# A two-layer streaming encoder in fp32: stage heads re-ordered, two projections finished by thirds of the tokens, last gate products on VectorE, four output buffers

## The chip, the cores and the metric

The kernel runs on one core of one Trainium2 chip. The metric is the device time of one execution in microseconds (us), taken as a median over several runs. The engines are TensorE (PE, its weight loads PEld), VectorE (DVE), ScalarE (ACT), GpSimd (POOL), and SyncE (SP), which only issues DMA here.

## The reference, cut to what matters

Two groups of tokens, 1024 of a new stream and 8 x 16 of running streams, are put side by side as 1152 columns and go through two layers with shared weights, d_model 1024, all in fp32.

```
for layer in range(2):
    h = rms_norm(x, norm_mix[layer])
    mix = ab_mixer(h, ...) if layer == 0 else chunk_mlp_mixer(h, ...)   # each ends in a projection to 1024
    x = x + mix
    h = rms_norm(x, norm_ffn[layer])
    a, gate = split(h @ w_in_ffn[layer])                                # 1024 -> 2 x 2816
    x = x + (gelu(causal_dwconv3(a)) * gate) @ w_out_ffn[layer]         # 2816 -> 1024
y = rms_norm(x, norm_final)
```

The outputs are y for both groups, and the recurrent, pooling and convolution states.

## The kernel before, in words

**Layout.** x lies transposed: eight tiles `xs[:, d, :]` (d = 0 to 7) of 128 channels by 1152 tokens. Token columns are cut into thirds of 384 (tb = 0 to 2) for the projections and into halves of 576 (T1S, T2S) for the feed-forward part. Every fp32 product is made of three fp32r products: an operand is split by ACT into a high part (a copy, `high`, `up_high`, `combo_high`, `w_high`, `y_high`) and by DVE into a low part (a subtraction, `low`, `up_low`, `combo_low`, `w_low`, `y_low`), and TensorE does high x high, high x low and low x high. So each weight piece and each data tile passes through ACT and then DVE before TensorE can use it.

**Order of the work.** There is no scheduler: each engine has a program written out by hand, runs it strictly in order, and waits on counting semaphores. An instruction that waits holds up everything behind it on its engine. SP issues all loads and stores in one such order too.

**Stages.** (1) mixer AB; its output projection is the stage "abo": tiles d = 0 to 5 are done whole (`abo_unit`, all three thirds, three matmuls to a weight block) and tiles 6 and 7 by thirds (`abo_group(d, tb)`, called by `by_token_block`, L1062 on). (2) `ffn(0)`. (3) stage "v" (`v_group`), then the u units, which alternate with `down` steps of mixer C; the last two pairs of channels go through `last_down` (stage "u9"): tiles 0 to 3 whole, tiles 4 to 7 by thirds (`group(d, tb)`, 12 matmuls of 384 columns each, L1054). (4) `ffn(1)`. (5) the final norm, one 128-token tile after another (`finish`, `final`, `store_out`), through two buffers `otok`.

**The end of a projection and the head of ffn.** For each finished group DVE adds the bank to `xs` (`add_down`, L1775), ACT squares it (`tail_sq`), and POOL adds the square to a sum (`add_square`, L3610). `norm_block(l, tb, ssq)` sums over partitions on TensorE (L1078; for tb 1 and 2 the last tile's square is added there, L1082), and ACT makes the reciprocal root (`rms`, L2824 and L2827). With blocks 0 and 1 known, DVE multiplies T1S by it (`normed`, L2239), and forms operands. The ffn is a Strassen-like scheme: 7 products instead of 8 for each pair of blocks, for the up part in 22 pairs n (`head_product(pos)`, pos 0 to 13, for the first two, `product` for the others; 24 matmuls of 288 columns each, L1524), for the down part in 7 products j of 11 steps (`down_step(r, f)`, r = 0 to 76, L1605). The head needs from DVE the sums and low parts of the seven x operands (`combo_sum` L2257, `combo_low` L2264), the weights' sums and low parts (`up_sum`, `up_low` L2235, in a ring of three places that come free with f_done), and the first bank evictions (`head_evict`, among them c22, L2291). The old x is stored to `x_scratch` in DRAM before `normed` overwrites it (waits on x_moved, x_moved_late) and is read back in the down part.

**From the up part to the down part.** A product gelu(conv) x gate of two 128 x 1152 blocks is made by POOL for every two pairs (`y_prod(i)`, i = 0 to 10, L3754), and SP stores it (`store_y(i)`, L791) and later reads halves of it back as y operands (`y_tiles`, L847). `step_weights(r)` (L843) loads the weights of step r, eight places in rotation. The last two products (i = 10) can be made only after the last up product; SP waits for them in `store_y(STEPS - 1)` at r = 6.

**Stage v.** `v_group(c, r)` multiplies 8 weight pieces k with three token tiles; for c = 0 pieces 6 and 7 go to places `va`, which lie over `xs` tile 0, so ACT waits for xl_ready before it writes them (L2811). The norm sums (`norm(2, ssq_v)`) stand behind `v_group(0, 0)`.

## Time and profile before

| | us |
|---|---|
| median of the three runs shown | 2722.01 (2717.48, 2722.01, 2722.22) |
| the profiled execution, its own time | 2718.93 |
| its span, first to last instruction | 2717.2 |
| PE busy in it | 2641.2, 97% |
| DVE, ACT, POOL busy | 1852.8 (68%), 938.0 (35%), 392.4 (14%) |
| mean granted TensorE clock | 0.993 of 2.4 GHz |
| DMA | 249 MB, mean 92 GB/s |

TensorE is busy for all but 76 us of the span. A view by windows of 1 us shows where the rest lies: 6.5 us at the start, stretches of 1 to 4 us around 504 to 555, 1020 to 1068, 1288, 1931 to 1973 and 2438 to 2487, and the last 23 us, in which it has only transposes.

### The profile page before, as it was taken

To read this page: it belongs to the slowest core of one execution; us is meant where nothing else is said; L and a number is where in the kernel's file an instruction comes from. 1 tells how busy PE (TensorE), PEld (TensorE's weight loads), DVE (VectorE), ACT (ScalarE), POOL (GpSimd) and SP (SyncE) were. 2 spreads that over 40 slices of the span, in tenths; PEclk is the share of its full clock that TensorE was granted. 3 is DMA by queue.
4 is the path that set the end of the run, shared out by engine and by line. 5 is a ranking of instruction groups with operands and counts; after the bars stand their busy time and mean duration, and the time that the engine had idled before them with its cause. 6 is when DMAs were issued, how large, how long until landed. Compare 5 with 4: busy or idle time off the path is not lost. (4 is left out here: it accounts for less than half of the span.)

```text
span 2717.2 us, 45387 instructions
## 1 busy us (share of the span) xinstructions
PE 2641.2 (97%) x17820; PEld 2567.2 (94%) x17820; DVE 1852.8 (68%) x3057; ACT 938.0 (35%) x1550; POOL 392.4 (14%) x299
## 2 busy tenths in 40 slices
PE   9999999899999998999999999999899999999998
PEld 8999999899999998999888999999899999999997
DVE  3558883687677778789223765555787777677787
ACT  4414553433232333445222221222532323334443
POOL 3134324201010100000000331001201111110000
PEclk9999999999999999999999999999999999999999
DMA  5111001322222337633111111111222222338533
GB/s 152 39 32 55 25 21 47 108 61 82 65 87 69 107 129 260 226 125 118 40 52 58 36 44 40 42 42 52 96 77 82 65 82 73 108 135 284 196 128 128
DMA packets 233346, 249.01 MB, mean 92 GB/s; under 512 B 13179, under 2 KB 171332, under 8 KB 232900
## 3 DMA queue, kind: packets, MB, share of 16 engines
q1 hardware_dynamic: 233124, 246.36, 27.8%
q8 instruction: 132, 2.16, 0.3%
q14 instruction: 58, 0.48, 0.1%
q10 hardware_dynamic: 32, 0.01, 0.0%
HBM read 202.12 MB, written 44.20 MB: 91 GB/s over the span
## 5 line engine op out<-in xcount | busy, mean ns | idle before, releaser
L1524 PE MATMUL banks<-cx,fh 128*128 128x288 f32 x2816 | 488.1, 295 | 8.8 <-ACT fh L3239 6.4
L1524 PEld LDWEIGHTS banks<-cx,fh 128*128 128x128 f32 x2816 | 413.1, 189 | 11.3 <-ACT fh L3239 7.8
L1524 PE MATMUL banks<-cw,fh 128*128 128x288 f32 x2112 | 368.3, 296 | 12.4 <-issue 6.1
L1524 PEld LDWEIGHTS banks<-cw,fh 128*128 128x128 f32 x2112 | 312.6, 190 | 13.7 <-issue 6.9
L1524 PE MATMUL banks<-cx,fl 128*128 128x288 f32 x1408 | 303.4, 297 | 0.0
L1605 PE MATMUL banks<-ysh,fh 128*128 128x288 f32 x1232 | 264.4, 296 | 17.0 <-DVE ysl L2410 13.2
L1605 PE MATMUL banks<-ysl,fh 128*128 128x288 f32 x1232 | 262.6, 294 | 0.0
L1605 PE MATMUL banks<-ysh,fl 128*128 128x288 f32 x1232 | 262.5, 294 | 0.0
L3754 POOL TENSOR_TENSOR gate<-gate,cv 128x1152 f32<-128x1152 f32 x44 | 120.6, 2742 | 926.3 <-DVE gate L2321 618.5
L3239 ACT ACTIVATE fh<-fraw 128x512 fp32r<-128x512 f32 x220 | 138.3, 631 | 319.1 <-PE banks L1524 264.6
L1524 PE MATMUL banks<-cw,fl 128*128 128x288 f32 x1056 | 228.8, 298 | 0.0
L1524 PEld LDWEIGHTS banks<-cx,fl 128*128 128x128 f32 x1408 | 225.4, 189 | 0.0
L1605 PEld LDWEIGHTS banks<-ysh,fh 128*128 128x128 f32 x1232 | 196.2, 188 | 20.3 <-issue 11.9
L2235 DVE TENSOR_TENSOR fl<-fraw,fh 128x512 fp32r<-128x512 f32 x220 | 152.4, 694 | 82.9 <-ACT fh L3239 82.9
L2803 ACT ACTIVATE wh<-raw 128x512 fp32r<-128x512 f32 x110 | 69.3, 630 | 403.2 <-PE banks L987 220.9
L1605 PEld LDWEIGHTS banks<-ysl,fh 128*128 128x128 f32 x1232 | 196.8, 188 | 0.0
L1605 PEld LDWEIGHTS banks<-ysh,fl 128*128 128x128 f32 x1232 | 196.6, 188 | 0.0
L1755 DVE TENSOR_TENSOR wl<-raw,wh 128x512 fp32r<-128x512 f32 x110 | 88.1, 801 | 125.3 <-ACT wh L2803 125.3
L1524 PEld LDWEIGHTS banks<-cw,fl 128*128 128x128 f32 x1056 | 170.2, 190 | 0.0
L1775 DVE TENSOR_TENSOR xs<-banks,xs 128x384 f32<-128x384 f32 x192 | 95.7, 550 | 91.2 <-PE banks L1012 46.1
L3604 POOL TENSOR_TENSOR raw<-raw,vec 128x512 f32<-128x512 f32 x72 | 84.8, 1183 | 461.2 <-DMA raw<-in_w_uv_c 380.8
L3305 ACT ACTIVATE fh<-flf 128x512 fp32r<-128x512 f32 x110 | 69.6, 633 | 212.0 <-DVE flf L2393 211.8
(417 smaller groups left out, 5312.1 us busy)
## 6 DMA issues: line engine op xcount, KB each, us to landing
fraw<-in_w_out_ffn SPq DMA_DIRECT2D x264, 256.0 KB, 3.4
fraw<-in_w_in_ffn SPq DMA_DIRECT2D x176, 256.0 KB, 4.1
y_scratch<-gate SPq DMA_DIRECT2D x44, 576.0 KB, 2.8
raw<-in_w_uv_c SPq DMA_DIRECT2D x64, 256.0 KB, 2.7
yb<-y_scratch SPq DMA_DIRECT2D x10, 1440.0 KB, 8.7
raw<-in_w_in_ab SPq DMA_DIRECT2D x40, 256.0 KB, 2.9
raw<-in_w_out_c SPq DMA_DIRECT2D x32, 256.0 KB, 2.6
x_scratch<-xs SPq DMA_DIRECT2D x10, 576.0 KB, 6.6
```

Source lines behind the costliest of these rows:

```text
L1524: mm = pe.matmul(bank[:, M0 + c * CH:M0 + (c + 1) * CH], w[:, pos % RING, k * P:(k + 1) * P], x[:, m, part, c * CH:(c + 1) * CH], start=fi ...
L1605: mm = pe.matmul(psp[f][:, M0 + c * CH:M0 + (c + 1) * CH], w[:, f * P:(f + 1) * P], x[:, r % RINGD, c * CH:(c + 1) * CH], start=kk == 0 an ...
L1755: dve.tensor_tensor(wl[:, s % 2, :], raw[:, s % RAWS, :], wh[:, s % 2, :].bitcast(F32), ALU.subtract)\
L1775: dve.tensor_tensor(xs[:, d, tbs(tb)], ps[sg % BANKS][:, 0:TB], xs[:, d, tbs(tb)], ALU.add)\
L2235: dve.tensor_tensor(fl[:, pos % RING, :], src, fh[:, pos % RING, :].bitcast(F32), ALU.subtract)\
L2803: act.activation(wh[:, s % 2, :], raw[:, s % RAWS, :], ACT.Copy).then_inc(w_high_ready, 1)
L3239: act.activation(fh[:, pos % RING, :], src, ACT.Copy).then_inc(f_high, 1)
L3305: act.activation(hi, src, ACT.Copy).then_inc(f_high, 1)
L3604: pool.tensor_tensor(r, r, g, ALU.mult).then_inc(w_scaled, 1)
L3754: pool.tensor_tensor(gate[:, c, :], gate[:, c, :], cv[:, c, :], ALU.mult)\
```

## The change

- Stage abo: tiles 0 to 4 whole, tiles 5, 6 and 7 by thirds. Stage u9: all eight tiles by thirds, so each group (d, tb) takes both parts a = 0 (yh4, yl4) and a = 1 (yh3, yl3) in turn.
- The weights of these groups get places of their own (`tail_place`), and squares four buffers instead of eight.
- Stores of old x: tiles 0 and 1 earlier, the tail tiles of a third in one store, in u9 all eight tiles a third.
- Head of ffn: DVE's and ACT's orders are changed (below), `up_sum` well ahead of its `up_low`.
- The last two gate products move from POOL to DVE, at r = 5 and 8; `store_y(STEPS - 1)` from r = 6 to 12, the read of y blocks 20 and 21 from r = 9 to 14.
- Stage v: pieces 6 and 7 of c = 0 go to new places `ve`, without the wait for xl_ready; the added squares come later, and `norm(2, ssq_v)` moves into `v_group(0, 1)` before k = 5.
- The end: four buffers `otok`; tiles in the order 5, 6, 7, 8, 0 to 4; the transposes of the first three stand between the last down steps of f = 1, 2, 3.
- POOL no longer forwards w_scaled piece by piece in abo and u9, and restores `xs` (xh + xl) two tiles at a time, done by tile 2.

```diff
 PLAN.add("ab", 40, 60, 80)
-PLAN.add("abo", 16, 24, 30)
+PLAN.add("abo", 16, 24, 29)
...
 PLAN.add("uu", 4, 6, 8)
-PLAN.add("u9", 8, 24, 26)
+PLAN.add("u9", 8, 24, 24)
...
-            return ((vb_h, vb_l) if c else (vd_h, vd_l), (wh, wl), (vc_h, vc_l), (va_h, va_l))[k // 2], k % 2
+            return (((vb_h, vb_l), (wh, wl), (vc_h, vc_l), (va_h, va_l)) if c else
+                    ((vd_h, vd_l), (wh, wl), (vc_h, vc_l), (ve_h, ve_l)))[k // 2], k % 2
 
         V_TILES = (6, 7, 8, 3, 4, 5, 0, 1, 2)
         V_SQUARES = tuple((d, 1) for d in range(KD)) + tuple((d, 0) for d in (4, 5, 6, 7, 0, 1, 2, 3))
-        SUMMED_SQ = {0: 18, 1: 48}
-        TAKEN_SQ = {0: 18, 1: 50}
-        TAIL_D = {0: 6, 1: 4}
+        SUMMED_SQ = {0: 15, 1: 36}
+        TAKEN_SQ = {0: 15, 1: 38}
+        TAIL_D = {0: 5, 1: 0}
         V_SUMMED, V_TAKEN = 22, 24
...
+            if l:
+                box, e = (tail_c, i) if i < 3 else (tail_b, i - 3) if i < 7 else (tail_a, 0)
+            else:
+                box, e = (tail_b, i) if i < 4 else (tail_a, i - 4)
+            return box[:, e, 0, :], box[:, e, 1, :]
 
         def v_added(s):
 
...
+            def store_x(d):
+
+                sp.wait_ge(acc_free, PLAN.at["abo"][1] + NTB * (d + 1))
+                sp.dma_start(xscr[0][d], xs[:, d, :]).then_inc(x_moved, 16)
...
-                for d in range(first):
-                    sp.wait_ge(acc_free, g0 + NTB * (d + 1))
-                    sp.dma_start(xscr[l][d], xs[:, d, :]).then_inc(x_moved, 16)
-                sp.wait_ge(pe_tick, t0 + (14 if l else 24))
+                if l == 0:
+                    for d in range(2, first):
+                        store_x(d)
+                sp.wait_ge(pe_tick, t0 + (0 if l else 20))
                 pair_blocks(1)
                 if l:
                     sp.wait_ge(pe_tick, PLAN.at["u9"][2])
...
+                back = xscr[l].rearrange("d p t -> p d t")
+                for a, b in ((0, 1), (1, 2), (2, 3)) if l else ((0, 2), (2, 3)):
+                    sp.wait_ge(acc_free, g0 + NTB * first + b * (KD - first))
+                    sp.dma_start(back[:, first:KD, a * TB:b * TB], xs[:, first:KD, a * TB:b * TB])\
+                        .then_inc(x_moved_late if b == NTB else x_moved, 16)
                 for n in range(2, PAIRS):
                     if n < 4:
...
-                    if r == 6:
+                    if r == 12:
                         store_y(STEPS - 1)
                     if r == 7:
                         y_tiles(yb22[:, 5:9, :], 16, 20, T2S, y_back[2])
                     if r == 20:
                         store_tails(l)
-                    if r == 9:
+                    if r == 14:
                         sp.wait_ge(y_saved[0], 16 * 12 * (l + 1))
-                        y_tiles(yb22[:, 9:11, :], 20, 22, T2S, y_back[2])
+                        y_tiles(yb22[:, 9:11, :], 20, 22, T2S, y_back[0])
                     if r in (13, 15):
                         d = r - 13
-                        sp.wait_ge(x_moved, 176 * l + 144)
+                        sp.wait_ge(x_moved, x_moves(l, X_STORES[l] + 1))
                         sp.dma_start(xs[:, d:d + 2, :], xscr[l][d:d + 2].rearrange("d p t -> p d t"))\
...
+                def group(d, tb):
+
+                    e = KD * tb + d
+                    q, dd = divmod(d, 2)
+                    acc_bank(g + e, g + e)
                     for a, (sh, sl) in enumerate(parts):
-                        if q == 0:
+                        if e == 0:
                             pe.wait_ge(yh_ready, done - 2 + 2 * a)
                             pe.wait_ge(yl_ready, done - 2 + 2 * a)
                         pe.wait_ge(w_high_ready, n + 2 * q + a + 1)
                         pe.wait_ge(w_low_ready, n + 2 * q + a + 1)
...
-
-                def group(d, tb):
-
-                    e = 12 + 4 * tb + d - 4
...
             def abo_group(d, tb):
 
-                e = 18 + 2 * tb + d - 6
+                e = 15 + 3 * tb + d - 5
...
+            def finish(i):
+
+                t = FIN_TILES[i]
+                if i < 4:
+                    pe.wait_ge(d_out, 28 + 24 + i + 1)
+                else:
+                    pe.wait_ge(y_out, i - 3)
+                for d in (4, 5, 6, 7, 0, 1, 2, 3):
+                    if i == 4 and d < 4:
+                        pe.wait_ge(d_out, 28 + 24 + d + 1)
+                    mm = pe.transpose(psp[i % 4][:, d * P:(d + 1) * P], xs[:, d, t * P:(t + 1) * P], ident[:, :])
+                mm.then_inc(fin_turned, 1)
             def ffn(l):
...
+                            if l and j == 6 and last == STEPS and f:
+                                finish(f - 1)
 
...
+                    if c == 0 and r == 1 and k == 5:
+                        norm(2, ssq_v)
                     (high, low), place = v_place(c, k)
...
             v_group(0, 0)
             pe.wait_ge(d_out, 28)
-            norm(2, ssq_v)
 
             def mixing_matrix(m):
...
-                at_first(2, first, KD - 1 - l)
+                at_first(2, first, 3 if l else 6)
                 dve.wait_ge(rstd_ready, NTB * 2 * l + 2)
-                dve.wait_ge(x_moved, 176 * l + 16 * KD)
+                dve.wait_ge(x_moved, x_moves(l, X_STORES[l]))
                 for d in range(4):
                     normed(d, T1S)
-                at_first(2, KD - 1 - l, KD - 1)
-                combo_low(0, 0)
-                combo_low(0, 1)
-                at_first(2, KD - 1, KD)
-                combo_low(0, 2)
-                combo_low(0, 3)
+                for k in range(4):
+                    combo_low(0, k)
+                    if l and k in (1, 3):
+                        at_first(2, 3 + k // 2, 4 + k // 2)
+                    if l == 0 and k == 1:
+                        at_first(2, 6, 7)
                 normed(4, T1S)
                 normed(5, T1S)
+                if l == 0:
+                    at_first(2, 7, 8)
                 combo_low(2, 0)
+                if l:
+                    at_first(2, 5, 6)
                 normed(6, T1S)
                 combo_low(2, 1)
+                if l:
+                    at_first(2, 6, 7)
                 normed(7, T1S)
                 combo_low(2, 2)
+                if l:
+                    at_first(2, 7, 8)
                 combo_low(2, 3)
                 up_low(3)
                 dve.wait_ge(rstd_ready, NTB * (1 + 2 * l))
-                dve.wait_ge(x_moved_late, 96 if l else 32)
+                dve.wait_ge(x_moved_late, 16 * (l + 1))
                 for d in range(4, KD):
                     normed(d, T2S)
+                up_sum(4)
                 dve.wait_ge(convc_mm, l + 1)
                 for k in range(4):
                     combo_low(6, k)
-                up_sum(4)
                 up_low(4)
+                up_sum(5)
                 for d in range(4):
                     normed(d, T2S)
+                up_low(5)
                 combo_sum(4, 2)
...
+                combo_sum(3, 3)
+                up_low(6)
                 for k in range(4):
                     combo_low(3, k)
-                for pos in (6, 7):
-                    up_sum(pos)
-                    up_low(pos)
+                up_sum(7)
                 for k in (0, 1, 3):
                     combo_sum(4, k)
+                up_low(7)
                 for k in range(4):
                     combo_sum(1, k)
+                up_low(8)
                 for k in range(4):
                     combo_low(4, k)
-                for n in range(2):
-                    head_evict(n, "d")
-                    up_low(8 + n)
+                head_evict(0, "d")
+                up_low(9)
                 for k in range(4):
                     combo_sum(5, k)
+                head_evict(1, "d")
+                up_low(10)
                 for k in range(4):
                     combo_low(1, k)
-                for n in range(2):
-                    head_evict(n, "a")
-                    up_low(10 + n)
+                head_evict(0, "a")
+                up_low(11)
+                head_evict(1, "a")
                 for k in range(4):
                     combo_low(5, k)
                 up_low(12)
-                up_low(13)
                 dve.memset(apad_a[:, 0:2], 0.0)
                 dve.memset(apad_b[:, 0:2], 0.0)
-                up_evict(10)
+                head_evict(0, "c22")
+                up_low(13)
+                head_evict(0, "c12")
                 for pos in range(12, UPS):
                     if pos + 2 < UPS:
                         up_sum(pos + 2)
...
-                conv_part(STEPS - 1, 1, 1)
+
+                def last_product(o):
+
+                    c = conv_half(STEPS - 1, o)
+                    dve.wait_ge(gelu_done[l], 2 * (STEPS - 1) + o + 1)
+                    if o:
+                        dve.wait_ge(up_act_out, on_act(l, PAIRS - 1, C11))
+                    dve.wait_ge(up_dve_out, on_dve(l, PAIRS - 1, (C21, C12)[o]))
+                    dve.tensor_tensor(gate[:, c, :], gate[:, c, :], cv[:, c, :], ALU.mult).then_inc(y_formed[l], 1)
                 for r in range(2, DOWNS):
                     j, kk = divmod(r + 1, STEPS)
...
+                    if r < 5:
+                        conv_part(STEPS - 1, 1, r - 1)
+                    if r in (5, 8):
+                        last_product(r // 8)
...
+                    v_low(V_N + 6)
+                    v_low(V_N + 7)
                     for s in range(8, 16):
                         x_low(s)
-                        if s > 8:
-                            add_square(s)
-                        if s == 13:
-                            v_low(V_N + 6)
-                            v_low(V_N + 7)
+                    for s in range(9, 16):
+                        add_square(s)
...
-            u_groups(7, 1, g3 + 3, t3 + 6)
             n2, g2, t2 = PLAN.at["u9"]
-            low(n2 + 1, n2 + 1)
+            tail_low(1, n2, 0)
+            u_groups(7, 1, g3 + 3, t3 + 6, lambda: tail_low(1, n2 + 1, 1))
+            tail_low(1, n2 + 2, 2)
             y_low(7, yh3, yl3)
-            finish_down(n2, g2, t2)
+            for i in range(3, 8):
+                tail_low(1, n2 + i, i)
...
+                if d == 4:
+                    act.wait_ge(xs_init, KD)
+                    for i in range(6):
+                        tail_high(0, n0 + 10 + i, i)
...
                         x_high(s)
-                    for s in range(10, 14):
-                        v_square(s)
-                    act.wait_ge(xl_ready, 24 + 14)
                     v_high(V_N + 6, 0)
                     v_high(V_N + 7, 0)
-                    v_square(14)
-                    v_square(15)
+                    for s in range(9, 16):
+                        v_square(s)
...
-                    u_gelu((p - 3) // 2, g3)
+            u_gelu(0, g3)
+            act.wait_ge(yl_ready, 12)
+            tail_high(1, n2, 0)
+            tail_high(1, n2 + 1, 1)
+            u_gelu(1, g3)
+            tail_high(1, n2 + 2, 2)
             uy_high(7, yh3)
-            n2, g2, t2 = PLAN.at["u9"]
-            finish_down(n2, g2, t2)
+            act.wait_ge(pe_tick, t2)
+            act.preload_act_table_set("natural_log_exp_and_others")
+            for i in range(3, 8):
+                tail_high(1, n2 + i, i)
...
+            pool.wait_ge(w_scaled, n0 + 4)
+            pool.sem_inc(w_scaled, 12)
+            for d in range(5):
+                for tb in range(NTB):
+                    e = NTB * d + tb
+                    add_square(e, e, sq_e[:, e % 2, :], tb, ssq_e)
+                if d < 3:
+                    restore(2 * d + 2)
+                    restore(2 * d + 3)
...
-                for i in range(STEPS):
+                for i in range(STEPS - 1):
```

## Rows read from the trace of the kernel before

**Rows 1.** The page, costliest groups: DVE's adds of projection groups.
```profile
L1775 DVE TENSOR_TENSOR xs<-banks,xs 128x384 f32<-128x384 f32 x192 | 95.7, 550 | 91.2 <-PE banks L1012 46.1
```

**Rows 2.** Waits of PE, 1008 to 1075: total us, times, longest.
```profile
PE banks L1605 <- DVE ysl L2410: 5.7, 3, 2.1
```

**Rows 3.** Waits of PE, 2430 to 2490.
```profile
PE banks L1605 <- DVE ysl L2410: 5.1, 3, 2.6
```

**Rows 4.** Timelines of DVE, POOL and SP, 1008 to 1072: start, us, what.
```profile
1018.09 3.21 DVE L2410 TENSOR_TENSOR ysl<-yb,ysh 128x576 fp32r<-128x576 f32 x1
...
1017.71 2.96 POOL L3754 TENSOR_TENSOR gate<-gate,cv 128x1152 f32<-128x1152 f32 x1 [31.24 <-DVE gate L2321]
...
1027.37 8.29 SPq L791 DMA_DIRECT2D y_scratch<-gate  x2
```

**Rows 5.** Timelines of ACT, PE and DVE, first head, 500 to 575.
```profile
500.28 1.15 ACT L3239 ACTIVATE fh<-fraw 128x512 fp32r<-128x512 f32 x2 [6.89 <-DMA fraw<-in_w_in_ffn]
...
507.18 0.91 PE L1078 MATMUL banks<-ssq_e,ones 128*128 128x384 f32 x2 [2.34 <-POOL ssq_e L3610]
...
512.74 0.69 PE L1511 MATMUL banks<-ident,crow 128*128 128x128 f32 x4
...
574.80 0.69 PE L1524 MATMUL banks<-cx,fh 128*128 128x288 f32 x4
...
509.95 3.01 DVE L2239 SCALAR_TENSOR_TENSOR xs<-xs,vec,rstd 128x576 f32<-128x576 f32 x4 [3.52 <-ACT rstd L2827]
...
522.88 3.00 DVE L2239 SCALAR_TENSOR_TENSOR xs<-xs,vec,rstd 128x576 f32<-128x576 f32 x4
...
567.81 0.28 DVE L2291 TENSOR_TENSOR apad_b<-banks,u 128x128 f32<-128x128 f32 x1
```

**Rows 6.** Waits of DVE in the first head, 509.9 to 569.
```profile
DVE fl L2235 <- ACT fh L3239: 3.1, 5, 0.7
```

**Rows 7.** Timelines of PE, DVE and POOL, second head, 1919 to 1994.
```profile
1922.77 0.91 PE L1078 MATMUL banks<-ssq_b,ones 128*128 128x384 f32 x2 [0.58 <-POOL ssq_b L3610]
...
1930.43 0.69 PE L1511 MATMUL banks<-ident,crow 128*128 128x128 f32 x4
...
1993.55 0.69 PE L1524 MATMUL banks<-cx,fh 128*128 128x288 f32 x4
...
1926.94 3.80 DVE L2239 SCALAR_TENSOR_TENSOR xs<-xs,vec,rstd 128x576 f32<-128x576 f32 x4
...
1927.66 1.01 POOL L3610 TENSOR_TENSOR ssq_b<-ssq_b,sq_t 128x384 f32<-128x384 f32 x1 [3.25 <-ACT sq_t L3179]
```

**Rows 8.** Windows: us, then PE, PEld, DVE, ACT, POOL busy (count), clock, DMA, GB/s.
```profile
600.00:650.00 50.00, 50.00 (x381) 50.00 (x380) 36.39 (x59) 15.28 (x23) 5.42 (x2) 1.00 0.21 67
...
1700.00:1750.00 50.00, 50.00 (x288) 50.00 (x287) 25.61 (x46) 9.89 (x16) 4.16 (x4) 1.00 0.14 42
...
1290.00:1295.00 5.00, 4.95 (x15) 3.94 (x16) 3.28 (x5) 0.92 (x2) 0.00 (x0) 0.66 0.34 108
...
1921.00:1926.00 5.00, 4.42 (x22) 3.57 (x21) 0.56 (x1) 2.88 (x6) 2.57 (x3) 1.00 0.80 315
```

**Rows 9.** Timelines of DVE and PE where stage u9 begins, 1880 to 1886.
```profile
1881.14 2.62 DVE L2730 TENSOR_TENSOR yl<-work,yh 128x1152 fp32r<-128x1152 f32 x2
...
1883.86 0.76 PE L1036 MATMUL banks<-yh,wh 128*128 128x384 f32 x3 [0.47 <-issue]
```

**Rows 10.** Timeline of PE, stage v, 1284 to 1298.
```profile
1290.05 0.47 PE L1647 MATMUL banks<-va_h,xh 128*128 128x512 f32 x1 [2.18 <-ACT va_h L2811]
```

**Rows 11.** Timelines of PE, ACT and DVE, the end, 2690 to 2717.
```profile
2693.89 3.96 PE L1744 MATMUL banks<-ident,xs 128*128 128x128 f32 x32
...
2695.27 1.03 ACT L3414 ACTIVATE fin_sq<-banks 128x1024 f32<-128x1024 f32 x1 [11.69 <-PE banks L1744]
...
2696.80 1.02 ACT L3414 ACTIVATE fin_sq<-banks 128x1024 f32<-128x1024 f32 x1
...
2712.88 1.28 DVE L2565 SCALAR_TENSOR_TENSOR otok<-banks,fin_sums,fin_gain 128x1024 f32<-128x1024 f32 x1 [1.13 <-DMA out_y_prompt<-otok]
```

More of the change, by code:

```diff
@@ L109, in build @@
         tails_stored = sem("tails_stored")
-        vout_stored = sem("vout_stored")
-        y_stored = [sem(f"y_stored{i}") for i in range(2)]
+        y_stored = [sem(f"y_stored{i}") for i in range(4)]
         w_scaled = sem("w_scaled")
```

305 lines of the change are left out of this document (121 added, 184 removed).

## The prediction, made before the changed kernel was run

> **What bounds the kernel.** The table's busy shares come first: TensorE is busy 97% of the span, so a change can win only what lies in its 76 us of idle time, in windows at half clock, and in the tail without matmuls. The windows of 1 us then say where the idle time is, and the waits and timelines say which instruction ended each stretch. The change touches five places.
>
> *Going down in ffn.* TensorE waits 5.7 us in three stalls in the first ffn and 5.1 in the second [rows 2, 3]. In the first stall DVE's low part of a y operand is started at 1018.09 and ends at 1021.30, just after POOL's gate product of 1017.71 to 1020.67 [rows 4]: the two don't run side by side. The other two stalls follow SP: it is held for 8.29 us from 1027.37 in the store of the last products [rows 4], with the weights of step 7 and on queued behind it.
>
> *The heads of ffn.* In the first, weight pieces of pair 1 come late, ACT waits 6.89 us for them to 500.28, DVE's adds of groups stand behind that, and TensorE waits 2.34 us before norm block 1 [rows 5]. From the end of the projection (E = 512.74, where the tap transposes begin) to the start of product 14 (574.80) it takes 62.1 us [rows 5]; 14 products of 24 matmuls at 50 us for 380 are 44.2 us [rows 8]. DVE is busy nearly all that time and is the bound; it is itself idle 3.1 us in five waits for ACT's high part between its sum and its low part [rows 6]. The second head is alike: E = 1930.43, product 14 at 1993.55, 63.1 us, after a wait of 0.58 us [rows 7].
>
> *Stage v*: 2.18 us of waiting for a high part of weights [rows 10], and then half clock. *The end*: the first transposes start at 2693.89, the last output tile is made at 2712.88 to 2714.16 [rows 11].
>
> **The clock.** The granted clock over 1290 to 1295 is 0.66, a fall to the 1.2 GHz level for part of it, after the 2.18 us idle; it costs 5 x (1 - 0.66) = 1.7 us [rows 8, 10]. Where DVE is the bound such a fall is hidden, elsewhere it adds.
>
> **Part by part.**
>
> *Last gate products to DVE, stores later.* POOL is gone from the place, SP is not held at r = 6. The three stalls go: 5.7 + 5.1 = 10.8 us. DVE gets two more products, each as long as two 576-column operations, at 3.01 for four [rows 5] 1.5 us; it has slack there, as one step of TensorE is 24 matmuls, 3.16 us [rows 8], and its own three operations take under 2.3. The stall on the tail rows' copies is untouched. If DMA were the limit the second and third stalls would return: bounds 10.8 and 3.2 (the first stall alone, 1.6 twice). I take 10.8, since the eight weight places give four steps, 12.6 us, for a load.
>
> *First head.* The tail is 9 groups of 24 matmuls of 384 columns, at 50 us for 288 each 4.17 us [rows 8], and norm block 1 stands two groups before E, not one. The weights of pair 1 load after tile 4, long before they are needed: 2.34 us saved. Norm block 1 at E - 8.3, add, square, two ACT operations: `normed` can start at E - 5.9, against 509.95 = E - 2.8 before. From there to the T2S multiplications DVE took 12.9 us [rows 5]; less the one wait of 0.3, plus one more add of 0.5 [rows 1], plus 0.7 for two square additions of POOL now beside it, 13.8: they start at E + 7.9. From there to the end of c22 it took 568.09 - 522.88 = 45.2 us [rows 5]; less the other waits, 2.8 [rows 6] and 0.1, and `up_low(13)`, 0.6, now behind it, 41.7. Product 12 starts there, product 14 6.3 us later: E + 55.9 against E + 62.1. With the 2.3, 8.5 us. Bounds: 5 if only the start moves, 11 if nothing of POOL is felt.
>
> *Second head.* All 24 groups by thirds, 12 matmuls, 2.08 us each; norm block 1 stands seven groups before E. `normed` can start when (2, 2) is added, E - 9.8. DVE's way to T2S is 12.9 - 0.3 plus four more adds, 14.6. But five square additions of POOL, 1.01 us each, now fall into it. Before, one made four multiplications take 3.80 instead of 3.01 [rows 5, 7], another cost about half of that; I take 0.6 each, 3.0. The add of (7, 2), 1.4 before the end of this, is done at E + 6.4. Only then can the last third of all eight tiles be stored, 1.57 MB, as much as moved in 1921 to 1926 [rows 8]: 4.6 us with the issue, and DVE waits for it before T2S: E + 11.0. Then 41.7 and 6.3: E + 59.0 against 63.1, 4.1; with the 0.6 of norm block 1, 4.7 us. Bounds: 7.5 without POOL's interference, 1.5 with a store of 6.6 us and full blocking.
> The Trainium skill (SBUF — State Buffer, Who interferes with whom) says that a VectorE instruction with two SBUF inputs and a GpSimd one that reads SBUF exclude each other for the whole instruction. The pair at 1018 agrees. By that rule each addition costs DVE its whole 1.01 us, five cost 5.0, and the sum below would be 2.0 lower.
>
> *Entry of u9.* What is new and bad: before, TensorE did 36 matmuls with yh4 (6.25 us, at 50 for 288 [rows 8]) before it needed yh3 and yl3, which are finished at 1881.14 + 2.62 = 1883.76, and waited 0.47 [rows 9]. Now the first group has 6 such matmuls, 1.04 us, and then waits in order for the same pair; one `tail_high` and one `tail_low` of some 0.6 (less than the 0.75 of 576 columns [rows 5]) stand in that way too, one leaves it. So 6.25 - 1.04 + 0.47, and 0.6 on top: a wait of 6.3 us, 5.8 more, and a fall of the clock, 1.7: -7.5 us. Bounds -4.5 (part of the work earlier, no fall) and -9.
>
> *Stage v.* The wait of 2.18 goes and with it the fall: 3.9 us. The x lows of T1S end about 1 us before `v_group(0, 1)` needs them. The norm is ten microseconds later; the first bank is evicted some 0.7 us before `v_group(0, 2)` wants it. Bounds 2.5 and 4.
>
> *The end.* ACT's pitch is 1.53 us a tile [rows 11], DVE's pair of buffers made it 2 (it waited 1.13 for a store [rows 11]). Tile 0 of the new order reaches ACT at about 2692.1, tiles 1 and 2 at 2694.7 and 2697.3 between the down steps, the other six follow at 1.53: the last output tile ends 3.0 us after ACT starts it (its own 1.53, DVE's 1.28, and 0.2 between), at 2709.6 against 2714.2: 4.6 us. Bounds 3 and 5.5.
>
> *At nothing:* restores, w_scaled, `x_scratch` stores of abo, the loop of u units. They lie under TensorE's full stretches (12.5 us a tile against 9 us of POOL), and would show as a wait in abo if that cover were too short.
>
> **The sum.** 10.8 + 8.5 + 4.7 - 7.5 + 3.9 + 4.6 = 25.0 us. The profiled execution took 2718.9, the median is 2722.0, two of the three runs near 2722 and one at 2717.5; 2693.9 and 2697.0. I predict 2695.5. About 0.2%, 5.4 us, can be told from no change.
>
> **Rivals.**
> 1. *DMA is the limit going down.* The last stores, the read-backs and the x reads now lie within r = 12 to 15. For: a load behind them waits longer, and there is a ceiling somewhere, with 0.80 of the DMA engines busy at 315 GB/s [rows 8]. Against: four steps of lead. It leaves 3.2 of 10.8: 25.0 - 7.6 = 17.4, some 2703.
> 2. *The full lock between POOL and DVE,* in the second head: 23.0, some 2697.5.
> 3. *The heads start no earlier,* because a store of old x or an order on ACT holds `normed`: only DVE's waits go, 3 us each, plus 2.9 before E: 25.0 - 13.2 + 8.9 = 20.7, some 2699; if the second head's store then costs its 4.6 on top, 2704.
> 4. *The new wait in u9 stays small*: if what it waits for is finished sooner, half of 7.5 comes back: 29, some 2692.
> 5. *Slower.* The clock falls in the 6.3 us wait of u9 and does not rise again in the stage. Its 288 matmuls, 50 us, would take 100: 25.0 + 1.7 - 50 = -23, some 2719 + 23 = 2742. It decides from some 64 us at the lower level. Against: after the 2.18 us in stage v the low clock lasted only part of 5 us [rows 8]; no gap of 6 us is in the trace.
> 6. *No change*: an order written wrongly somewhere, with a wait of its own that eats 20 us or more; nothing in the profile points to it, and all orders meet TensorE at 97%.
>
> **Chances.** The forecast 0.52, rival 1 0.12, 2 0.12, 3 0.09, 4 0.07, 5 0.03, 6 0.05. The range takes in the bounds of the parts (three of them low together, 14 us) and rivals 1 to 4: 2686 to 2708. Faster 0.91, same 0.05, slower 0.04.
>
> **What would show it.** No stall of L1605 on y operands or late weights; POOL without a gate product after 1017; the first product right after the tap transposes; DVE's waits for fh gone; product 14 at E + 56 and E + 59; a wait of about 6 us in L1054's successor at the start of u9, with a fall of the clock; no wait in stage v; tiles at a pitch of 1.5 us in the end. The forecast is wrong if TensorE's idle time stays near 76 us, or if a wait of over 3 us stands anywhere but at u9's start.

## The result, and the profile after

The changed kernel takes 2694.84 us, the median of four runs (2692.55 to 2697.69), against 2719.74 for the kernel before in the same comparison; the ratio is 0.9909, with a 95% interval of 0.9892 to 0.9927. The forecast was 2695.5, in a range of 2686 to 2708. Its profiled execution took 2696.33 us with a span of 2694.5, so 22.7 us of span are to be explained, where the sum said 25.0.

The page of the changed kernel, its span and its busy times (us, share of the span, instructions):

```profile
span 2694.5 us, 45383 instructions
PE 2633.9 (98%) x17820; PEld 2563.1 (95%) x17820; DVE 1851.1 (69%) x3061; ACT 938.4 (35%) x1550; POOL 381.3 (14%) x295
```

TensorE's time without work falls from 76.0 us to 2694.5 - 2633.9 = 60.6 us; the other 7.3 us of the gain are busy time, and the mean granted clock is 0.995 instead of 0.993, so less of the work ran at the lower level.

A sum of terms is best read by landmarks that both kernels have. The table takes the stretches between them from the times of TensorE's instructions in the timelines of the two profiled executions; the forecast column is the terms of the prediction.

| stretch | before | after | difference | forecast |
|---|---|---|---|---|
| start to the projection of abo | 420.7 | 423.8 | +3.0 | 0 |
| to E, the tap transposes | 92.0 | 89.4 | -2.6 | -2.3 |
| E to product 14 | 62.1 | 56.0 | -6.1 | -6.2 |
| rest of the up part | 445.2 | 445.5 | +0.4 | 0 |
| down part of ffn(0), with the step into it | 255.5 | 248.4 | -7.1 | -5.7 |
| stage v and the u units | 601.7 | 597.8 | -3.9 | -3.9 |
| u9, to the second E | 53.3 | 59.8 | +6.5 | +6.9 |
| E to product 14 | 63.1 | 60.7 | -2.5 | -4.1 |
| rest of the up part | 445.2 | 445.6 | +0.4 | 0 |
| down part of ffn(1) and the end | 278.4 | 267.6 | -10.8 | -9.7 |

The sum is -22.7. The +3.0 in the first row stands in code that the change doesn't touch: in the profiles of all 13 other kernels of this case (that before among them) the projection of abo starts between 419.7 and 423.2, here at 423.8. The two +0.4 do belong to the change. They are one wait of TensorE, 13 to 14 us behind the start of product 14, in the first and the second up part; before, it was 0.5 in each:

```profile
PE banks L1542 <- issue: 0.8, 1, 0.8
PE banks L1542 <- issue: 1.0, 1, 1.0
```

The trace names no releaser; in both kernels the first matmul behind it starts 0.1 us after DVE ends a low part of weights (L2228 at 582.01, 0.68 us long, before the matmul at 582.80). So DVE is still the bound there, and the forecast of 0 for this row missed a small term.

**Going down.** Waits of TensorE in the changed kernel, 1008 to 1070 and 2420 to 2480 (total us, times, longest); in [rows 2, 3] stood three stalls on L1605 in each:

```profile
PE banks L1623 <- ACT trow L3231: 1.7, 1, 1.7
...
PE banks L1505 <- DVE xs L2423: 0.3, 1, 0.3
```

What is left in both is the wait for the tail rows, as foretold, and in the second ffn a new one of 0.3 us for DVE's `xs` in front of the transposes. POOL has no instruction between 1000 and 1075, so the gate products are gone from it.

**The first head.** Timelines of PE and DVE, to be laid beside [rows 5]:

```profile
513.14 0.69 PE L1529 MATMUL banks<-ident,crow 128*128 128x128 f32 x4
...
569.10 0.69 PE L1542 MATMUL banks<-cx,fh 128*128 128x288 f32 x4
...
506.19 3.00 DVE L2232 SCALAR_TENSOR_TENSOR xs<-xs,vec,rstd 128x576 f32<-128x576 f32 x4 [1.91 <-ACT rstd L2852]
...
521.08 3.01 DVE L2232 SCALAR_TENSOR_TENSOR xs<-xs,vec,rstd 128x576 f32<-128x576 f32 x4 [0.34 <-ACT rstd L2852]
...
562.03 0.29 DVE L2284 TENSOR_TENSOR apad_b<-banks,u 128x128 f32<-128x128 f32 x1
```

The multiplications of T2S start at E + 7.9, c22 ends at E + 49.2 and product 14 starts at E + 56.0; foretold were 7.9, 49.6 and 55.9. `normed` starts at E - 7.0, a microsecond sooner than the E - 5.9 of the working, and the stretch behind it takes that much longer (14.9 us instead of 13.8): two errors that cancel. DVE's waits for ACT's high parts, five of 3.1 us together in [rows 6], are down to one:

```profile
DVE fl L2228 <- ACT fh L3252: 0.7, 1, 0.7
```

**The second head.** PE, DVE and POOL, beside [rows 7]:

```profile
1920.56 0.69 PE L1529 MATMUL banks<-ident,crow 128*128 128x128 f32 x4
...
1981.22 0.69 PE L1542 MATMUL banks<-cx,fh 128*128 128x288 f32 x4
...
1910.83 3.81 DVE L2232 SCALAR_TENSOR_TENSOR xs<-xs,vec,rstd 128x576 f32<-128x576 f32 x4
...
1926.86 0.55 DVE L1785 TENSOR_TENSOR xs<-banks,xs 128x384 f32<-128x384 f32 x1
...
1933.35 3.00 DVE L2232 SCALAR_TENSOR_TENSOR xs<-xs,vec,rstd 128x576 f32<-128x576 f32 x4 [3.18 <-DMA x_scratch<-xs]
...
1911.55 1.02 POOL L3634 TENSOR_TENSOR ssq_b<-ssq_b,sq_t 128x384 f32<-128x384 f32 x1 [1.07 <-ACT sq_t L3210]
```

DVE begins at E - 9.7 (foretold E - 9.8), the last add is done at E + 6.9 (6.4), T2S starts at E + 12.8 (11.0) and product 14 at E + 60.7 (59.0). The store of the last third was down 5.9 us behind the add, not 4.6.

**The entry of u9 and stage v.** PE and DVE, then windows from 1861 on and from 1290, with the granted clock ahead of the last two numbers:

```profile
1868.15 0.66 PE L1059 MATMUL banks<-yh,tail_c 128*128 128x384 f32 x1 [6.29 <-DVE yl L2750]
...
1865.42 2.63 DVE L2750 TENSOR_TENSOR yl<-work,yh 128x1152 fp32r<-128x1152 f32 x2 [0.36 <-ACT yh L3563]
...
1861.00:1872.00 11.00, 4.71 (x19) 4.42 (x19) 9.03 (x14) 7.75 (x12) 0.00 (x0) 0.69 0.24 73
1865.00:1868.00 3.00, 0.00 (x0) 0.00 (x0) 2.64 (x3) 2.97 (x4) 0.00 (x0) 0.50 0.27 87
1868.20:1871.40 3.20, 3.20 (x10) 3.20 (x11) 2.50 (x4) 1.74 (x4) 0.00 (x0) 0.50 0.24 80
1871.50:1874.00 2.50, 2.50 (x16) 2.50 (x15) 1.48 (x3) 0.92 (x2) 0.00 (x0) 1.00 0.03 7
1290.00:1295.00 5.00, 5.00 (x31) 4.07 (x30) 0.00 (x0) 2.94 (x8) 0.00 (x0) 1.00 0.00 0
```

The new wait is there with 6.29 us, where 6.3 was foretold. The clock is at the 1.2 GHz level, half of full speed, which a window shows as 0.50. So 0.69 over 11 us means 2 x 11 x (1 - 0.69) = 6.8 us at that level. About half of them lie inside the wait, which ends at 1868.15, and cost nothing. In the 3.3 us behind it, to 1871.5, ten matmuls start 0.32 us apart instead of 0.17: 1.6 us, near the 1.7 of the working. Then the clock is back at full speed, as it came back in the kernel before. In stage v nothing waits and the clock stays up.

**The end.** The first and the last tile on ACT and DVE:

```profile
2673.76 1.03 ACT L3435 ACTIVATE fin_sq<-banks 128x1024 f32<-128x1024 f32 x1 [8.21 <-PE banks L1518]
...
2687.88 1.02 ACT L3435 ACTIVATE fin_sq<-banks 128x1024 f32<-128x1024 f32 x1
...
2678.73 1.28 DVE L2576 SCALAR_TENSOR_TENSOR otok<-banks,fin_sums,fin_gain 128x1024 f32<-128x1024 f32 x1
...
2690.19 1.28 DVE L2576 SCALAR_TENSOR_TENSOR otok<-banks,fin_sums,fin_gain 128x1024 f32<-128x1024 f32 x1
```

DVE makes its first output 5 us after ACT's first square, since it has down evictions to do till then, and then goes from tile to tile in 11.46 / 8 = 1.43 us without a wait for a store. ACT's pitch is 1.53, as foretold, but with that late start it is DVE that bounds the end: each output follows the one before it at once.

### The profile page after: what moved, and what is told of

It reads as the page before. It is cut to its first block, busy times and chain, and to the rows that moved or that the text cites. A ratio compares the mean times of both kernels' runs of the same rounds, so it can differ in the third digit from the quotient of the medians.

```text
span 2694.5 us, 45383 instructions
## 1 busy us (share of the span) xinstructions
PE 2633.9 (98%) x17820; PEld 2563.1 (95%) x17820; DVE 1851.1 (69%) x3061; ACT 938.4 (35%) x1550; POOL 381.3 (14%) x295
## 4 chain that ended last, share of the span: by engine, by line
PE 86%; DVE 9%; issue 2%; ACT 1%; DMA 1%; DVEq 0%; POOL 0%; SPq 0%; ACTq 0%; POOLq 0%
PE banks L1542 34%; PE banks L1623 15%; PE banks L1011 10%; PE banks L1669 7%; PE banks L1036 6%; PE banks L1189 3%; PE banks L1059 2%; PE banks L1475 1%; PE banks L1494 1%; PE banks L1224 1%; PE banks L1127 1%; DVE xs L2423 1%; PE banks L1728 1%; DVE xs L2232 1%; DMA fraw<-in_w_out_ffn 1%
## 5 line engine op out<-in xcount | busy, mean ns | idle before, releaser
L3767 POOL TENSOR_TENSOR gate<-gate,cv 128x1152 f32<-128x1152 f32 x40 | 108.3, 2708 | 827.0 <-DVE gate L2314 556.3
L2228 DVE TENSOR_TENSOR fl<-fraw,fh 128x512 fp32r<-128x512 f32 x220 | 152.7, 695 | 77.8 <-ACT fh L3252 77.8
```

The costliest lines, as they stand in the source:

```text
L2228: dve.tensor_tensor(fl[:, pos % RING, :], src, fh[:, pos % RING, :].bitcast(F32), ALU.subtract)\
L3767: pool.tensor_tensor(gate[:, c, :], gate[:, c, :], cv[:, c, :], ALU.mult)\
```

## The experiments

Ratios are against the kernel before in the same comparison. Its median moved between 2719.3 and 2721.6 from one comparison to the next, so a difference between two changed kernels is uncertain by some 2 us; where a microsecond matters, the stretch of the table is read, in one profile of each.

**1. u9's first groups (u9six).** Parts a = 0 of six groups first, weight pieces loaded in that order:

```diff
+        LAST_PIECES = ((0, 0), (1, 0), (2, 0), (0, 1), (1, 1), (2, 1), (3, 0), (3, 1))
...
+                    if e == 0:
+                        for f in range(6):
+                            acc_bank(g + f, g + f)
+                            half(f, 0, 0)
+                    if e > 5:
+                        acc_bank(g + e, g + e)
+                        half(d, tb, 0)
+                    half(d, tb, 1)
```

> The changed kernel with stage u9 opened as before the change in substance: the a = 0 parts of the first six groups of block 0 (36 matmuls, which need only yh4 and yl4) stand ahead of their a = 1 parts, and the weight pieces are loaded in that order. Theory (the stall of 6.3 us is the order alone): 36 matmuls cover 6.25 us, yl is finished at the same time as now, and the fourth weight piece one subtraction later, so a wait of about 2 us stays, without a fall of the clock: 4.3 + 1.7 = 6.0 us less than the changed kernel, some 2689. Rival A (the operands themselves come later than before, or the fourth piece's load is the late one): the wait stays over 3 us, the gain is under 3 us. Rival B (what is won here is waited for again in the second head, since DVE bounds it and its start depends on the last adds): the wait goes but the total moves by less than 1 us.

2690.85 us, ratio 0.9887 (0.9870 to 0.9903). PE in the place of the wait, and the window:

```profile
1865.36 0.41 PE L1060 MATMUL banks<-yh,tail_c 128*128 128x384 f32 x1 [0.23 <-DVE tail_c L2178]
...
1869.42 0.41 PE L1060 MATMUL banks<-yh,tail_b 128*128 128x384 f32 x1 [1.70 <-DVE tail_b L2178]
...
1861.00:1872.00 11.00, 9.07 (x51) 8.49 (x51) 9.18 (x14) 7.73 (x11) 0.00 (x0) 1.00 0.24 73
```

Two waits of 1.93 us together, no fall; u9 takes 54.2 us instead of 59.8, 5.6 less where 6.0 was expected: the stall was the order alone. Of this 4.4 is waiting; the 1.2 left is the 1.6 of the clock, less what two short waits cost beyond their idle time. The median is 4.0 lower, by the ratios it would be 6; neither is better than the stretch.

**2. The last store of old x in two (split).**

```diff
+                    for d0, d1 in ((4, KD), (0, 4)) if l and b == NTB else ((first, KD),):
+                        sp.dma_start(back[:, d0:d1, a * TB:b * TB], xs[:, d0:d1, a * TB:b * TB])\
+                            .then_inc(x_moved_late if b == NTB and d1 == KD else x_moved, 16)
...
+                if l:
+                    dve.wait_ge(x_moved, x_moves(l, 3))
                 for d in range(4):
                     normed(d, T2S)
```

> The changed kernel with the last store of old x in the second ffn cut in two, tiles 4 to 7 first and tiles 0 to 3 behind it; the four multiplications of T2S that come first wait only for the first half. Theory (DVE's wait of 3.2 us for that store is on the path of the second head, and the store's time is its bytes): half the bytes are down some 2.5 us sooner, DVE waits under 1 us, product 14 starts 2 to 2.5 us sooner against the tap transposes, and the total falls by 2 to 2.5 us. Rival (the time is latency and issue, not bytes): the wait falls by under 1 us and the total doesn't move.

2692.66 us, ratio 0.9894 (0.9878 to 0.9911). DVE in the second head:

```profile
1932.09 3.01 DVE L2233 SCALAR_TENSOR_TENSOR xs<-xs,vec,rstd 128x576 f32<-128x576 f32 x4 [0.94 <-DMA x_scratch<-xs]
```

The wait falls from 3.18 to 0.94, product 14 stands at E + 58.4 instead of 60.7: 2.2 us, and the median moved by as much, which by itself is no more than its scatter. Half the bytes hold DVE till 3.7 us behind the last add (1928.38 to 1932.09), all of them 5.9. So most of the store's time goes with its bytes; by these two points some 1.5 us would not (an estimate).

**3. Both.** The two together, and the fourth piece's high part ahead of ACT's table load.

> Both edits together, and ACT makes the high part of the fourth weight piece of u9 ahead of its table load. If the two are independent and the first is order alone: 6.0 + 2.3 + some 0.5 to 1 = about 9 us less than the changed kernel, near 2686; under 7 would say that one hides the other.

2685.77 us, ratio 0.9870 (0.9854 to 0.9886): 9.1 us under the changed kernel by the medians, where about 9 was expected. u9 takes 53.7 us, 6.1 less, E to product 14 58.5, 2.2 less. The two add up.

**4. What POOL's additions cost (nosq).** The kernel leaves out seven sums of squares. It ran once, in 2690.45 us; only stretches are read. In the second head, for the last block:

```diff
+                        if l and tb == 2:
+                            pool.wait_ge(square_ready, TAKEN_SQ[l] + s + 1)
+                            pool.wait_ge(ssq_added, added)
+                            pool.tensor_tensor(ssq[:, 768:776], ssq[:, 768:776], sq_t[:, s % 4, 0:8], ALU.add)\
+                                .then_inc(ssq_added, 1)
```

> The changed kernel, leaving out seven sums of squares of the last block in the second head: POOL adds 8 columns instead of 384 there, so the root for the last block is wrong. It measures what POOL's additions cost DVE. In the changed kernel the stretch of DVE from its first multiplication of T1S to the end of the last add is 16.6 us (1910.83 to 1927.41), with five additions of 1.0 to 1.6 us on POOL in it, 5.9 us together. As I predicted (0.6 us each): 13.6. Full exclusion (each blocks DVE for its whole length): 10.7 to 11.5. No interference: 16.6. The total should move little, since DVE waits for the store of old x behind it.

DVE's first multiplications, its last add and the wait behind it:

```profile
1908.03 3.00 DVE L2232 SCALAR_TENSOR_TENSOR xs<-xs,vec,rstd 128x576 f32<-128x576 f32 x4
...
1921.10 0.55 DVE L1785 TENSOR_TENSOR xs<-banks,xs 128x384 f32<-128x384 f32 x1
...
1927.71 3.00 DVE L2232 SCALAR_TENSOR_TENSOR xs<-xs,vec,rstd 128x576 f32<-128x576 f32 x4 [3.30 <-DMA x_scratch<-xs]
```

The stretch is 1921.65 - 1908.03 = 13.6 us against 16.6: 3.0 us for five additions, 0.6 each on average, as in the sum. But the cost isn't spread evenly. In the changed kernel the four multiplications with one addition wholly beside them take 3.81 instead of 3.00, so that one costs 0.8 of its 1.02. Laid side by side, DVE's instructions in the two kernels differ by 0.8, 0.3, 0.8, 0.3 and 0.8 us at the five additions. The pair of [rows 4] stretched one subtraction over all of POOL's product, and DVE's adds from a bank take 0.55 beside POOL as without it:

```profile
1923.22 1.63 POOL L3634 TENSOR_TENSOR ssq_b<-ssq_b,sq_t 128x384 f32<-128x384 f32 x1 [2.39 <-ACT sq_t L3210]
...
1923.90 0.55 DVE L1785 TENSOR_TENSOR xs<-banks,xs 128x384 f32<-128x384 f32 x1
```

The Trainium skill (SBUF — State Buffer, Who interferes with whom) says that a VectorE instruction with at most one SBUF input, outside its two-port modes, doesn't contend with GpSimd; the adds agree. What is paid is overlap with work of two SBUF inputs. The 5.0 us that I worked out by that page in the prediction take every addition as lying wholly beside such work; here part of them lies beside adds and gaps, and even an addition wholly beside it cost 0.8 and not 1.0. One forecast on this run fell: I said that the total would move little since the store is waited for anyway. The store follows the last add, so it came sooner too: product 14 at E + 57.8 instead of 60.7. DVE still waits 3.30 us for it.

**5. Gate products back on POOL (poolprod).** `for i in range(STEPS)` in POOL's program, `last_product` left out.

> The changed kernel with the last two gate products of each ffn back on POOL, behind its other products; the store at r = 12 and all else stay. Theory (the first of the three stalls was POOL's product against DVE's low part, the other two were SP held in the store): the first stall comes back in both ffns, 1.6 us and some 0.3 us of slower first matmuls each, the other two don't; 3.5 to 4 us more than the changed kernel, all of it within the first microseconds after the last product. Rival (any of the three needs both parts of the edit): two or three stalls return, 7 to 14 us more. Rival (the stall was DVE's own load, not POOL): no difference.

**6. The kernel before with the store at r = 12 (bstore).**

```diff
-                    if r == 6:
+                    if r == 12:
                         store_y(STEPS - 1)
...
-                    if r == 9:
+                    if r == 14:
```

> The kernel before with the store of the last products moved from r = 6 to r = 12 and the read of y blocks 20 and 21 from r = 9 to r = 14 (with its own count); the products stay on POOL. Theory: stalls two and three go in both ffns, 4.1 and 3.5 us idle with some 0.7 us of slower matmuls behind each pair, the first stays at 1.6: 8 to 9 us less than before. Rival (DMA traffic was the limit, SP's wait only its sign): other waits of over 1 us for weights come within r = 8 to 20, and less than 4 us is won.

2698.97 us, ratio 0.9926 (0.9910 to 0.9943), and 2711.43, ratio 0.9970 (0.9960 to 0.9980). Waits of PE behind the last product of the first ffn, in poolprod and in bstore:

```profile
PE banks L1623 <- ACT trow L3229: 1.7, 1, 1.7
PE banks L1623 <- DVE ysl L2403: 1.6, 1, 1.6
```

```profile
PE banks L1605 <- ACT trow L3222: 1.7, 1, 1.7
PE banks L1605 <- DVE ysl L2410: 1.6, 1, 1.6
```

The three stalls of [rows 2] had two causes that don't touch: POOL's product against DVE's low part made the first (1.6 in each ffn, 4.1 us more by the medians when it is put back, as expected), SP held in the store made the others (7.9 us less when it is freed, where 8 to 9 were expected). No wait of 1 us for weights came in either, so DMA was not the limit.

**7. Stage v piece by piece (bve, bvn, bvall).** On the kernel before: the new places without ACT's wait; then the norm's sums moved on TensorE too; then DVE's lows ahead of its adds too.

```diff
+            return (((vb_h, vb_l), (wh, wl), (vc_h, vc_l), (va_h, va_l)) if c else
+                    ((vd_h, vd_l), (wh, wl), (vc_h, vc_l), (ve_h, ve_l)))[k // 2], k % 2
...
+                    if c == 0 and r == 1 and k == 5:
+                        norm(2, ssq_v)
...
                     for s in range(8, 16):
                         x_low(s)
-                        if s > 8:
-                            add_square(s)
+                    for s in range(9, 16):
+                        add_square(s)
```

> The kernel before with the last two weight pieces of c = 0 in stage v in the new places, without ACT's wait, and made earlier on ACT and DVE; the norm's sums stay where they were on TensorE. Theory (the stall of 2.18 us and the clock's fall behind it come from that wait alone): the stage's stall goes and the clock stays up, 3.5 to 3.9 us less than before. Rival (the move of the norm behind later matmuls was needed too): a wait of 1 to 3 us for the squares takes its place, and the gain is under 1.5 us.

> The run before this one with the new places (bve) and, in addition, the norm's sums moved on TensorE to where the change has them, into the second group of tiles ahead of its sixth weight piece. In bve the stall of 2.18 us was replaced by one of 2.65 us in front of the norm, for the squares. Theory (the two edits work only together): no wait over 0.3 us is left in the first 30 us of stage v, the clock stays up, and the stage up to the end of the u units takes 597.7 us as in the changed kernel instead of 601.7: 3.9 us less than before. Rival (the order of ACT's and DVE's squares, which the change moved too, is needed as well): a wait of 1 us or more for the norm or for the last block's operands stays, and less than 2.5 us is won.

> bvn with the third part of the change's stage v: DVE makes all eight low parts of the first halves of x before it adds the squares, instead of in turn. In bvn a wait of 2.23 us for such a low part stood in the place of the others. Theory (the three parts work only together): no wait over 0.3 us in stage v's first 30 us, and stage v to the end of the u units takes 597.7 us instead of 601.7, 3.9 us less than before. Rival (a fourth wait of about 2 us, since the load of the second of the two weight pieces is late: ACT waited 1.85 us for it): under 2 us is won.

Medians 2725.20, 2720.21 and 2717.32; ratios 1.0017 (1.0006 to 1.0027), 1.0000 (0.9990 to 1.0009) and 0.9991 (0.9982 to 1.0001). PE's timeline at the place, in bve and in bvn:

```profile
1298.11 0.88 PE L1098 MATMUL banks<-ssq_v,ones 128*128 128x384 f32 x2 [2.65 <-issue]
```

```profile
1297.48 0.77 PE L1652 MATMUL banks<-vd_h,xh 128*128 128x512 f32 x1 [2.23 <-DVE xl L2557]
```

The stage with the u units takes 601.7, 603.9, 601.8 and 597.7 us in before, bve, bvn and bvall. Under the wait of 2.18 for the places [rows 10] lay one of 2.65 for the squares, and under that one of 2.23 for a low part: my expectation fell for the first two steps, and the first alone is slower than nothing. The trace names no releaser for the 2.65 ("issue"), but DVE's last addition of a square ends at 1298.00, 0.1 us before TensorE goes on, and bvn, which moves only the sums, hasn't this wait. Only the three together give the 4.0, and that is shown by the stretch alone: the median of bvall is 2.2 under before, in an interval that reaches to no difference. The medians of these three scatter by more than 4, since they keep the late weights of the first head (below).

**8. The early transposes (noearly).** `finish(f - 1)` out of the last steps, all nine tiles behind them.

> The changed kernel with the first three tiles' transposes behind the last down step instead of between the last steps; order of the tiles and the four buffers stay. The prediction counted 1.5 to 2 us for starting early. The trace of the changed kernel says otherwise: DVE makes its first output only at 2678.7, behind its last eviction, since the transposes push the down steps back by 3 us, and then works back to back. Theory (early transposes bring nothing, the gain of the end is the four buffers and ACT's pitch): the end is within 0.5 us of the changed kernel's. Rival (they are worth what was predicted): 1.5 to 2 us more.

2694.64 us, ratio 0.9908 (0.9891 to 0.9925), no different from the changed kernel by the medians. By the stretches the down part and the end take 268.8 instead of 267.6: 1.1 us are lost. Some 0.4 of them are small waits in the middle of the down part, which come and go between profiles. Behind the last down matmul it takes 19.3 us instead of 16.8, and the transposes of two tiles had pushed the last steps back by 1.7. So the early transposes are worth 0.7 to 1.1, neither the 0.5 at most of the theory nor 1.5 to 2. DVE starts its outputs here 1.6 us behind its last eviction:

```profile
2675.71 0.76 DVE L2421 TENSOR_TENSOR xs<-xs,banks 128x576 f32<-128x576 f32 x1 [0.84 <-PE banks L1623]
2678.06 0.16 DVE L2568 RECIPROCAL fin_sums<-fin_sums 128x1 f32<-128x1 f32 x1 [1.59 <-ACT fin_sums L3436]
```

In the kernel before the end took 23.2 us behind the last down matmul, here 19.3, so 3.9 of the 5.1 us won at the end are the rest of that edit.

**9. DVE as the bound (headload).** Four sums of operand 5 made twice.

```diff
+                    if x == 5:
+                        dve.tensor_tensor(summed(x, k), a, b, ALU.subtract).then_inc(doubled, 1)
+                        dve.wait_ge(doubled, 4 * l + k + 1)
```

> The changed kernel with DVE's four sums of operand 5 made twice in each head (nothing else reads the first copies): some 3.0 us more of DVE's time per head, 0.7 to 0.75 each with a wait for its own result. Theory (DVE is the bound of both heads, and what lies behind it passes every microsecond on): product 14 starts 2.7 to 3.1 us later in both heads, and the total is 5.5 to 6 us more than the changed kernel. Rival (TensorE and ACT bound the end of the head, DVE has slack by then): product 14 moves by less than 1.5 us, the total by under 3.

2700.70 us, ratio 0.9925 (0.9908 to 0.9942): 5.9 us more, as expected. E to product 14 takes 59.3 and 63.6 us, 3.4 and 3.0 more. DVE bounds both heads; TensorE's waits there are its sign.

**10. Squares summed by TensorE (sqpe).** On `both`: POOL adds two squares of the last block, TensorE six.

```diff
+                        if l and tb == 2 and d in (4, 6, 7):
+                            take_square({4: 2, 6: 3, 7: 4}[d])
...
+                mm = pe.matmul(ps[6][:, 0:TB], ones[:, :], sq_t[:, s % 4, :], start=d == 2, stop=False,
+                               skip_group_check=True)
```

> The run of both edits (both), and in the second head POOL adds only the first two squares of the last block; TensorE sums the other six itself, with one matmul on ones for each, three of them before the tap transposes. Theory (the leaving-out run: what POOL's additions cost DVE beside its two-input work is 3.0 us, and TensorE has slack there): DVE's stretch from its first multiplication of T1S to the last add is 13.6 to 14.2 us instead of 16.6, product 14 starts 2.5 to 3 us sooner against the start of DVE's T1S work, and the total is 2 to 3 us under the run of both. Rival (the store of old x becomes the wait again, or TensorE's six matmuls of 0.3 to 0.6 us hold up the last groups and so DVE's adds): under 1 us.

2685.57 us, ratio 0.9872 (0.9852 to 0.9893), against 2685.77 for both: nothing, so the rival held. DVE:

```profile
1904.74 3.00 DVE L2267 SCALAR_TENSOR_TENSOR xs<-xs,vec,rstd 128x576 f32<-128x576 f32 x4
...
1917.82 0.55 DVE L1820 TENSOR_TENSOR xs<-banks,xs 128x384 f32<-128x384 f32 x1
...
1924.26 3.01 DVE L2267 SCALAR_TENSOR_TENSOR xs<-xs,vec,rstd 128x576 f32<-128x576 f32 x4 [1.86 <-ACT rstd L2889]
```

The stretch to the last add is 13.6 us as meant, but DVE then waits 1.86 us for the root, and 2.67 for ACT's `fh` where the changed kernel has 1.41. TensorE sums three squares before the tap transposes and the last ones behind them, at 0.64 us each, so that u9 is 2.0 us longer than in both. From u9's start to product 14 it takes 111.4 us, against 112.2 in both: 0.8 of the 3.0 is left.

## Why the prediction was right, and where its terms were off

- **Going down, 10.8 forecast.** ffn(0) gave 7.1 and ffn(1) 5.7 (before against noearly, which has no transposes in it: 255.3 - 249.6), together 12.8. The cause is confirmed for each stall by experiments 5 and 6, and rival 1 (DMA) fell. The term was too small since it counted only the idle time of the three stalls. Each cost 0.16 us beyond its idle time (from the start of the last matmul to the next one 1.90 us for a wait of 1.61, where 0.13 is usual), and a second small wait 2 us behind the first stall cost 0.3 in each ffn. This makes 1.5 of the 2.0; the rest I can't place. It isn't one lucky profile: the first down part takes 256.3 us on average in the four kernels that have all stalls (in two of them with a fall of the clock) and 249.4 in the eight that have none, 6.9.
- **First head, 8.5 forecast:** 2.6 + 6.1 = 8.7, its last landmarks within 0.4 us. That is closer than the working deserved: `normed` came 1.1 sooner and the stretch behind it was 1.1 longer.
- **Second head, 4.7 forecast:** 2.5, and the 0.6 of norm block 1 (inside u9's row). The start and POOL's 3.0 us were right [experiment 4], rival 2, the full lock for each addition, fell. The step that failed is the store, "as much as moved in 1921 to 1926 [rows 8]: 4.6 us with the issue": it took 5.9, 1.3 more, and the last add was 0.5 late, so product 14 came 1.7 us later. Rival 3 had the cause (a store of old x holds `normed`) but not the size.
- **Entry of u9, -7.5 forecast:** the wait was 6.29, against the foretold 6.3, and the clock's fall cost 1.6 behind it, against 1.7; experiment 1 gives back 5.6 of the two. The row shows 6.5; with the 0.6 of norm block 1, that is a cost of 7.1. Rivals 4 and 5 fell: the wait did not shrink, and the clock came back.
- **Stage v, 3.9 forecast:** 3.9. The size was right, but the reason given, that one wait goes, was one of three: the norm's move and DVE's order, which the change has too, were needed as well, and the prediction gave them no part in the term.
- **The end, 4.6 forecast:** 10.8 - 5.7 = 5.1, of which the early transposes are 0.7 to 1.1. The working let ACT's pitch of 1.53 bound it; DVE did, at 1.43 from its last eviction on.
- **Not in the sum:** +3.0 at the start, in this one execution, and +0.8 behind the heads, which stands in every kernel with the new heads in the second up part and in all but headload in the first. 25.0 forecast against 24.9 by the medians is partly luck: the going down gave 2 more than forecast, the second head nearly 2 less, and the two medians themselves are known to some 2 us only.

A part that I can only argue: the kernels that keep the old first head (before, bstore, bve, bvn, bvall) take 92.0, 94.9, 94.2, 94.9 and 92.0 us to E, the others 89.4 in every profile. The late weights [rows 5] cost 2.6 or, in three of the five, where the wait is longer and the clock falls behind it, up to 5.5; so the change may be worth some 1.6 us more on average there than the profile of before shows; with five profiles that is not shown.

## What to carry to other kernels

Read a wait that is to be removed for what is queued behind it on every engine: in stage v two more of about the same length lay underneath, and taking away the first alone made the kernel 0.17% slower. An order that lets each group run to its end needs its latest operand at once; put the parts that need only the early operand first, as the six opening groups of u9six do. And where an instruction waits for a store, store the half that it overwrites first.

## What was not expected of the hardware

- A stall costs more than its idle time even where the clock stays up: the stalls that went in the two down parts were 5.7 + 5.1 = 10.8 us idle, less 0.3 that is new, and the stretches fell by 12.8. Each stall cost some 0.16 us beyond its wait, and the pair of matmuls behind one shows 0.50 us instead of 0.43.
- A gap of 2.2 us was followed by a fall of the clock in some executions and not in others: the stall of stage v in before had one [rows 8], the same stall of 2.17 us in bstore had none (granted clock 1.00 from 1290 to 1296). In bstore the clock fell instead at 1027.5 (0.57 from 1027 to 1031), where the only wait just ahead was the 1.60 us of the first stall, to 1025.99.
- In the down part DVE's last evictions of the second product sometimes hold TensorE for 0.4 to 1.3 us, behind a weight load that DVE waited up to 3.5 us for (split). It shows in 10 of the 14 profiles, with the old order and with the new, but not in those of before and after themselves, so a difference of a microsecond between two down parts says little.
